# The second down-projection of a ConvFFN as seven block products per pair of output tiles

## The chip, the cores and the metric

One Trainium2 chip, one of its NeuronCores. The metric is the device time of one execution in microseconds (us); shown is the median of several runs. TensorE (PE) multiplies, VectorE (DVE), ScalarE (ACT) and GpSimd (POOL) work elementwise, SyncE (SP) issues most of the DMA transfers. The engines run side by side, each through its own program in order, and meet only at semaphores.

## The reference

One layer of a hybrid recurrent decoder with a convolutional feed-forward network, over 1056 tokens: a prompt of 1024 and 8 samples of 4. Everything is float32. What matters here is its end:

```python
h2 = modulate(h_res, p['g_ffn'], sh2, sc2)
up = h2 @ p['w_up']                                   # 1024 -> 2 x 2816
buf = jnp.concatenate([st_conv[layer], up], axis=1)
conv = causal_dwconv(buf, p['conv_w'], p['conv_b'], l) # three taps in time
a_ff, b_ff = jnp.split(conv, 2, axis=-1)
h_res = h_res + gt2[:, None, :] * ((jax.nn.gelu(a_ff) * b_ff) @ p['w_down'])   # 2816 -> 1024
...
y = rms_norm(h_res, final_g).astype(x.dtype)
```

## The kernel before

All activations are held transposed: channels on the 128 partitions, the 1056 tokens along the free dimension. Up to the end of the token mixers and the output projection the change touches nothing.

The feed-forward network runs in two halves over its 22 channel tiles of 128, `HALVES = ((0, 12), (12, 22))`. In each half, the up-projection makes for every step `r` one tile of `a_ff` and one of `b_ff`; the gated result is stored tile by tile in `FFh`. Then the down-projection adds this half's contribution to the residual. So the second half's down-projection has ten k tiles (channels 12 to 21).

The up-projection and the output projection are already done in blocks: a 2 x 2 block matrix product with seven block products in the place of eight (Winograd's form of Strassen's method). The weights of a step are four blocks A11 to A22 (two output tiles, two halves of the k tiles), the activations four blocks B11 to B22 (two halves of the k tiles, two halves of 528 tokens). VectorE makes the weight sums S1 = A21 + A22, S2 = S1 - A11, A11 - A21 (in the place of A21 in the weight slot) and S4 = A12 - S2 (`four_sums`), and the activation sums once for the whole stage. TensorE does the products in PSUM banks, taken in pairs, and VectorE and ScalarE combine them from there (`combined` in the up-projection). Each product is two groups of 264 columns.

The down-projection of both halves is done plainly: for each of eight output tiles, three token groups of 352 columns, each summed over the k tiles in one PSUM bank out of six (`gemm`). The first tile begins with the k tiles that are ready and ends with the last two (`gemm_from_early`), which the convolution of the last step still works on. VectorE adds each group to the residual with the gate (`residual`), and in the second half also accumulates the squares for the final norm and scales by its gain (`squares(2, m)`).

On VectorE, a step of the up-projection is: the convolution `conv(r-1, 0)` of the step before (three taps for 1024 prompt tokens, three for the 32 decode tokens), the combination of product 2, `conv(r-1, 1)`, which also multiplies with the GELU branch and signals `ff_ready`, then the combinations of products 4 and 5, weight sums for the next step around the latter, and the combinations of products 6 and 7. The two convolutions of a half's last step come behind its last combination. Its signals are counted: the banks of the last step's first and third product are free with the combination of product 6, those of its second with that of product 7.

Weights come in chunks through two slots of `W`. SyncE loads chunk i when TensorE has finished with chunk i - 2 (`weights`); a chunk of the second down-projection is 1280 KB and holds two output tiles. Behind the second of these chunks SyncE reloads the residual, eight tiles of 528 KB, from `xres` into `xT`, which shares its memory with the up-projection's activation sums.

Behind the last residual, TensorE sums the squares over the partitions (`sq3`, two planes, against a column of ones), VectorE and ScalarE make the reciprocal root, TensorE turns the tiles into rows, VectorE and ScalarE scale these out of PSUM, and SyncE stores them.

Every instruction of VectorE's `step` signals its end, and the engine waits for it. L718 is TensorE's matrix product helper, L722 its transposition, L2001 VectorE's tensor-tensor, L2004 its scalar-tensor-tensor, L2592 the first tap of the convolution, L2060 the scaling by the final gain, L439 SyncE's weight load, L536 its reload of the residual.

Of the kernel before, what the change touches and what calls it, by code (L numbers as in the profile page):

```python
# [15 lines left out]
P = 128  # L16
D = 1024
KT = D // P
# [3 lines left out]
T = TP + TS  # L22
# [3 lines left out]
G, GW = 3, T // 3  # L26
# [48 lines left out]
def weight_chunks():  # L75
# [10 lines left out]
    for m0, m1 in HALVES:  # L86
        out += [("up", m, 2 * PRODUCTS) for m in range(m0, m1, 2)]
        out += [("down", (m0, c), 2 * G) for c in range(4)]
    return out


def trunk(nc, I, O):
# [5 lines left out]
    with ctx:  # L98
# [160 lines left out]
        sq2, rstd2 = carve(18944, 2, T), carve(21056, T)  # L259
        sq3 = carve(21056, 2, T)  # L260

# [134 lines left out]
        def product(r, x):  # L396

            return signals[index[("up", 2 * (r // 2))]] + PRODUCTS * (r % 2) + x

        def slots(r):  # L400
# [302 lines left out]
        def _(pe):  # L703
# [790 lines left out]
            def last_rows(n):  # L1494
# [6 lines left out]
                give("conv_rows", 7)  # L1501

            def pair(r):

# [36 lines left out]
            for half, (m0, m1) in enumerate(HALVES):  # L1541
# [13 lines left out]
                pe.wait_ge(sem("ff_ready"), m1 - 2)  # L1555
                for c in range(4):
                    i = index[("down", (m0, c))]
# [34 lines left out]
        def _(act):  # L1592
# [359 lines left out]
            for m0, m1 in HALVES:  # L1952
# [18 lines left out]
                decode_rows(m1 - 1)  # L1971
                state_rows(m1 - 1)
            rows_out(FT // 2 - 1)
            root(rs9, 12)
# [9 lines left out]
        def _(dve):  # L1984
# [622 lines left out]
            dve.wait_ge(sem("x_in0"), 64 + 16 * KT)  # L2607
            def second_half(m, from_):

                gt, d = MOD[:, 16 + m, :], dec4(res_t[:])  # L2610
                x = xT[:, m, HT:TP]
                step(stt(x, from_[:, 0:TP - HT], gt[:, 0:1], x, MUL, ADD))
                step(tt(d, dec4(from_[:, TP - HT:HT]), gt[:, 1:].unsqueeze(2).to_broadcast([P, NS, LS]), MUL))
                return tt(xT[:, m, TP:T], xT[:, m, TP:T], res_t[:], ADD)

            def first_half(m, from_):
                x = in_two(xT[:, m, 0:HT])
                return stt(x, from_, MOD[:, 16 + m, 0:1], x, MUL, ADD)

# [50 lines left out]
            for half, (m0, m1) in enumerate(HALVES):  # L2670
                for r in range(m0, m1):
# [12 lines left out]
                    if r + 1 < m1:  # L2684
                        sums(r + 1, 2, 4)
                    combined(r, 6, c21, c21, x, SUB)
                    combined(r, 7, c12, c12, y, ADD)
# [7 lines left out]
                else:  # L2695
                    for k in range(2):
                        dve.wait_ge(sem(f"x_in{k}"), (320, 208)[k])
                    residual(signals[index[("down", (m0, 0))]], 40, 2)
            step(v.memset(rs9, 1.0))
# [47 lines left out]
```

## Time and profile before

| | |
|---|---|
| median of 3 runs | 2348.9 us |
| lowest and highest | 2346.8, 2354.57 us |
| profiled execution: its time | 2351.13 us |
| profiled execution: its span | 2349.4 us |
| mean granted clock of TensorE | 0.984 |
| busy: TensorE, VectorE, ScalarE, GpSimd | 2243.8, 1069.8, 403.0, 162.2 us |

The span is from the first to the last instruction of one execution; its time has some more around it. "Busy" is the sum of the intervals in which an engine works; several engines are busy at once. The granted clock is the share of TensorE's full clock that the chip let it have: 1.00 is 2.4 GHz, 0.50 is 1.2 GHz. In the timelines a line is a run of like instructions of one engine, merged, and the bracket behind it tells the idle time of its engine before it and what ended that.

### The profile page before, as it was taken

Reading aid. Unit: us, or ns where it says so; the run is one execution under the profiler, and the core shown is the slowest. Engines: PE = TensorE matmul, PEld = TensorE weight load, DVE = VectorE, ACT = ScalarE, POOL = GpSimd, SP = SyncE. Lnnn points to the kernel's source line nnn. Section 1 sums busy time; section 2 is a strip of 40 time slices with the busy share of each in tenths; the row PEclk is TensorE's granted clock in tenths of the full one; section 3 lists DMA queues with packets and bytes.
Section 4 is the critical chain, followed back from the end, with each engine's and each line's share of the span. In section 5 each row is a group of like instructions: output and inputs, shape, how many; then the busy total and the mean of one; then the engine's idle time right before and its main releaser. Section 6 shows DMA issues by size and latency. Waiting matters only on the chain.

```text
span 2349.4 us, 41778 instructions
## 1 busy us (share of the span) xinstructions
PE 2243.8 (96%) x18567; PEld 1601.7 (68%) x18567; DVE 1069.8 (46%) x1698; ACT 403.0 (17%) x775; POOL 162.2 (7%) x276
## 2 busy tenths in 40 slices
PE   5998999998999999899889998999999999999998
PEld 4665666566567566566656686888886668888666
DVE  5775334252353253234234656666652115566423
ACT  3124121231132042132110003111110001111001
POOL 2610000001002002001000000000000000000000
PEclk8999999999999999999999999999999999999999
DMA  8200232212021111211236322111112231110301
GB/s 315 79 23 11 65 123 88 72 47 57 20 67 32 49 31 51 63 37 47 69 112 213 101 74 73 37 38 38 38 60 77 82 109 38 37 39 24 119 23 75
DMA packets 117090, 161.52 MB, mean 69 GB/s; under 512 B 15442, under 2 KB 86599, under 8 KB 116896
## 3 DMA queue, kind: packets, MB, share of 16 engines
q1 hardware_dynamic: 101120, 132.68, 17.1%
q10 hardware_dynamic: 10992, 15.21, 1.8%
q0 software_dynamic: 4800, 10.97, 1.4%
q8 instruction: 147, 2.41, 0.4%
q14 instruction: 31, 0.25, 0.0%
HBM read 126.24 MB, written 32.59 MB: 68 GB/s over the span
## 4 chain that ended last, share of the span: by engine, by line
PE 92%; DMA 3%; ACT 2%; DVE 1%; issue 1%; SPq 1%; POOL 0%; DVEq 0%; ACTq 0%
PE ps L718 91%; DMA W<-in_w_in_dram 2%; PE ps L722 1%; ACT Y L1704 1%; DVE arena L2001 1%; SPq L424 1%; DVE hT L2001 0%; SPq L439 0%; DMA arena<-in_state_s_dram 0%; ACT hT L1906 0%; DMA out_dram<-arena 0%; ACT hT L1647 0%; DVE arena L2189 0%; ACT L1704 0%; SPq L443 0%
## 5 line engine op out<-in xcount | busy, mean ns | idle before, releaser
L718 PE MATMUL ps<-hT,W 128*128 128x352 f32 (+1 forms) x3376 | 1002.6, 447 | 26.9 <-DMA W<-in_w_in_dram 13.0
L718 PEld LDWEIGHTS ps<-hT,W 128*128 128x128 f32 x3376 | 632.9, 192 | 287.0 <-issue 23.1
L718 PE MATMUL ps<-arena 64*64 64x64 f32 (+8 forms) x9784 | 414.3, 240 | 37.2 <-issue 20.4
L718 PEld LDWEIGHTS ps<-arena 64*64 64x64 f32 (+4 forms) x9784 | 332.6, 138 | 166.7 <-issue 100.8
L718 PE MATMUL ps<-arena,W 128*128 128x352 f32 (+1 forms) x1600 | 439.4, 434 | 1.6 <-DVE arena L2001 1.6
L718 PEld LDWEIGHTS ps<-arena,W 128*128 128x128 f32 x1600 | 303.9, 190 | 131.2 <-issue 2.1
L2001 DVE TENSOR_TENSOR arena<-ps,arena 128x512 f32<-128x512 f32 (+4 forms) x124 | 93.2, 751 | 243.6 <-PE ps L718 199.1
L2001 DVE TENSOR_TENSOR Y<-Y,ps 128x528 f32<-128x528 f32 x130 | 91.6, 705 | 241.6 <-PE ps L718 241.5
L2001 DVE TENSOR_TENSOR arena<-arena 128x1056 f32<-128x1056 f32 (+6 forms) x178 | 159.9, 898 | 63.7 <-PE ps L718 48.9
L1602 ACT ACTIVATE Y<-ps 128x528 f32<-128x528 f32 (+1 forms) x92 | 37.5, 407 | 804.8 <-DVE Y L2001 293.3
L1602 ACT ACTIVATE arena<-ps 128x512 f32<-128x512 f32 (+6 forms) x143 | 86.9, 617 | 457.6 <-PE ps L718 269.1
L2004 DVE SCALAR_TENSOR_TENSOR arena<-ps,MOD,arena 128x352 f32<-128x352 f32 (+2 forms) x52 | 30.5, 587 | 241.5 <-PE ps L718 236.2
L650 POOL DMA_DIRECT2D out_dram<-arena x72 | 40.4, 567 | 1334.0 <-ACT arena L1602 1061.0
L718 PE MATMUL ps<-Y,W 128*128 128x352 f32 x384 | 114.7, 460 | 5.2 <-DVE Y L2001 2.7
L718 PEld LDWEIGHTS ps<-Y,W 128*128 128x128 f32 x384 | 72.6, 190 | 46.0 <-DVE Y L2001 3.2
L1730 ACT ACTIVATE arena<-ps 128x352 f32<-128x352 f32 x72 | 33.5, 465 | 323.0 <-PE ps L718 323.0
L671 POOL TENSOR_TENSOR arena<-arena,m_lt 128x512 f32<-128x512 f32 x40 | 50.4, 1267 | 399.0 <-DVE flag L2428 281.6
L2004 DVE SCALAR_TENSOR_TENSOR Y<-Y,PAR 128x1024 f32<-128x1024 f32 (+1 forms) x88 | 67.6, 768 | 3.1
L2004 DVE SCALAR_TENSOR_TENSOR arena<-Y,PAR,arena 128x1024 f32<-128x1024 f32 (+1 forms) x88 | 67.6, 768 | 3.1
L718 PEld LDWEIGHTS ps<-idS,arena 64*64 64x64 f32 (+1 forms) x1888 | 40.3, 134 | 26.1 <-issue 20.9
L718 PE MATMUL ps<-hT,arena 128*128 128x264 f32 x240 | 55.9, 386 | 0.0
L718 PEld LDWEIGHTS ps<-hT,arena 128*128 128x128 f32 x240 | 45.6, 190 | 7.8
(295 smaller groups left out, 1353.3 us busy)
## 6 DMA issues: line engine op xcount, KB each, us to landing
W<-in_w_ada_dram SPq DMA_DIRECT2D x12, 2048.0 KB, 9.6
W<-in_w_up_dram SPq DMA_DIRECT2D x22, 1024.0 KB, 7.1
W<-in_w_in_dram SPq DMA_DIRECT2D x13, 1024.0 KB, 6.3
gates<-arena ACTq DMA_DIRECT2D x72, 176.0 KB, 1.8
arena<-gates SPq DMA_DIRECT2D x24, 528.0 KB, 3.7
arena<-xres SPq DMA_DIRECT2D x24, 528.0 KB, 5.2
xres<-arena POOLq DMA_DIRECT2D x16, 528.0 KB, 5.8
W<-in_w_in_dram SPq DMA_DIRECT2D x13, 512.0 KB, 7.3
```

The source lines that it names most:

```text
L424: sp.dma_start(dst, src).then_inc(sem("small_in"), 16)
L650: pool.dma_start(dst, src).then_inc(sem(name), 16)
L671: pool.tensor_tensor(LT[:, 8 * s:8 * s + 8, :], LA[:, 8 * s:8 * s + 8, 0, :], m_lt[:, l, :].unsqueeze(1).to_broadcast([P, 8, RCH]), MUL)\
L718: return nc.tensor.matmul(out, lhsT, rhs, start=start, stop=stop, skip_group_check=True)
L722: return nc.tensor.transpose(out, in_, ident[0:n, 0:n])
L1602: return nc.scalar.activation(out, in_, ACT.Copy)
L1704: m = nc.scalar.activation(Y[q, j // 4, o::DS], src[32 * o:32 * o + 32, 0:M], ACT.Gelu_apprx_tanh)
L1730: nc.scalar.activation(stage, bank[:, 0:GW], ACT.Sigmoid).then_inc(sem("gate_ev"), 1)
L2001: return v.tensor_tensor(out, a, b, op)
L2004: return v.scalar_tensor_tensor(out=out, in0=a, scalar=s, in1=b, op0=op0, op1=op1)
```

## The change

The second half's down-projection is done in blocks as well. Its ten k tiles are two halves of five, its 1056 tokens two halves of 528, and each of the four weight chunks (two output tiles) is four blocks of 5 x 128 columns. Per chunk (a pair r) there are seven block products of five k tiles and two groups of 264 columns (`down_pair`).

- VectorE makes the activation sums once: FT1 = F12 - F11 and the first pair's four weight sums between the combinations of products 5 and 6 of the up-projection's last step; FT2 = F22 - FT1, FT3 = F22 - F12 and FT4 = FT2 - F21 (in the place of F12) behind the last two convolutions.
- TensorE's products in a pair: 1 A11 F11 (banks 0, 1), 2 S1 FT1 (banks 2, 3), 3 A12 F21 onto 1, 4 S2 FT2 (banks 4, 5), 5 (A11 - A21) FT3 (banks 0, 1), 6 A22 FT4 (banks 4, 5), 7 S4 F22 onto 2. Each waits for its sums and for the reader of its banks. F21 and F22 hold the last two channel tiles (`ff_ready`).
- ScalarE copies product 1 to SBUF (`p12_ev`). VectorE adds the products up and adds the results to the residual (`down_blocks_out`): u2 = product 1 + product 4, v = u2 + product 5, and so on, with the next pair's weight sums between them, and squares and scaling of the two tiles at the pair's end. In the last pair these are cut into halves of the tokens and ordered so that little follows the last product.
- The activation sums, weight sums and partial results lie in `hT`, which held the normed input of the up-projection, and in free parts of `Y` and the arena. `sq3` moves from the arena to `Y`.
- The chunks now count 7 signals instead of 6, so SyncE's loads wait for the seventh product of a pair.

The diff, its core:

```diff
--- before.py
+++ after.py
@@ -85,7 +85,7 @@
     out += [("out", c, 2 * PRODUCTS) for c in range(2)]
     for m0, m1 in HALVES:
         out += [("up", m, 2 * PRODUCTS) for m in range(m0, m1, 2)]
-        out += [("down", (m0, c), 2 * G) for c in range(4)]
+        out += [("down", (m0, c), PRODUCTS if m0 else 2 * G) for c in range(4)]
     return out
...
@@ -257,7 +257,7 @@
         cvr = carve(23168, 2, 512)
...
-        sq3 = carve(21056, 2, T)
+        sq3 = Yf[:, T:3 * T].rearrange("p (a b) -> p a b", a=2)
...
@@ -396,6 +396,25 @@
         def product(r, x):
 
             return signals[index[("up", 2 * (r // 2))]] + PRODUCTS * (r % 2) + x
+
+        KH = (HALVES[1][1] - HALVES[1][0]) // 2
+        five = lambda a: a.rearrange("p (k c) -> p k c", k=KH)
+        F11, F12, F21, F22 = (FFh[:, KH * a:KH * (a + 1), HT * b:HT * (b + 1)] for a in range(2) for b in range(2))
+        FT1a, FT1b = carve(21056, 4, HT), Yf[:, 7088:7088 + HT]
+        FT2, FT3, FT4 = five(hflat[:, 0:KH * HT]), five(hflat[:, KH * HT:2 * KH * HT]), F12
+        SD = [[five(a) for a in (carve(8448, KH * P), carve(8448 + KH * P, KH * P), Yf[:, 7616:7616 + KH * P])],
+              [five(hflat[:, 5280 + KH * P * i:5280 + KH * P * (i + 1)]) for i in range(3)]]
+        dpart = [hflat[:, 7200:7200 + HT], hflat[:, 7200 + HT:7200 + 2 * HT], Yf[:, 0:HT]]
+        S_DOWN, P12_DOWN, RES_DOWN = 16 + 4 * FT, 4 + 2 * FT, 28 + KT * G
+
...
@@ -1500,6 +1519,50 @@
...
+            def down_pair(r):
+
+                def multiply_down(b, A, B, first=True, last=True):
+                    for g in range(2):
+                        for k in range(KH):
+                            m = mm(pb[b + g][:, 0:HG], A[:, k, :], B(k)[:, HG * g:HG * (g + 1)],
+                                   first and k == 0, last and k == KH - 1)
+                    m.then_inc(sem("gemm_done"), 1)
+
+                arrived(index[("down", (HALVES[1][0], r))])
+                A11, A12, A21, A22 = down_blocks(r)
+                S1, S2, S4 = SD[r % 2]
+                of = lambda B: lambda k: B[:, k, :]
+                take(0, 1)
+                multiply_down(0, A11, of(F11), True, False)
+                pe.wait_ge(sem("s_sums"), S_DOWN + 4 * r + 1)
+                if r == 0:
+                    pe.wait_ge(sem("h_ready"), 5)
+                take(2, 3)
+                multiply_down(2, S1, lambda k: FT1a[:, k, :] if k < 4 else FT1b, True, False)
+                if r == 0:
+                    pe.wait_ge(sem("ff_ready"), FT)
+                pe.wait_ge(sem("p12_ev"), P12_DOWN + r + 1)
+                multiply_down(0, A12, of(F21), False, True)
+                pe.wait_ge(sem("s_sums"), S_DOWN + 4 * r + 2)
+                if r == 0:
+                    pe.wait_ge(sem("h_ready"), 6)
+                take(4, 5)
+                multiply_down(4, S2, of(FT2))
+                pe.wait_ge(sem("s_sums"), S_DOWN + 4 * r + 3)
+                if r == 0:
+                    pe.wait_ge(sem("h_ready"), 7)
+                pe.wait_ge(sem("res_ev"), RES_DOWN + 7 * r + 1)
+                multiply_down(0, A21, of(FT3))
+                if r == 0:
+                    pe.wait_ge(sem("h_ready"), 8)
+                pe.wait_ge(sem("res_ev"), RES_DOWN + 7 * r + 2)
+                multiply_down(4, A22, of(FT4))
+                pe.wait_ge(sem("s_sums"), S_DOWN + 4 * r + 4)
+                pe.wait_ge(sem("res_ev"), RES_DOWN + 7 * r + 4)
+                multiply_down(2, S4, of(F22), False, True)
+                for b, at in ((0, 3), (4, 5), (2, 6)):
+                    last_read[b] = last_read[b + 1] = ("res_ev", RES_DOWN + 7 * r + at)
+
...
@@ -1553,7 +1616,10 @@
...
                 pe.wait_ge(sem("ff_ready"), m1 - 2)
-                for c in range(4):
+                if half:
+                    for r in range(4):
+                        down_pair(r)
+                for c in range(0 if half else 4):
...
@@ -1970,6 +2036,11 @@
...
+            for r in range(4):
+                act.wait_ge(sem("gemm_done"), down_product(r, 1))
+                if r:
+                    act.wait_ge(sem("res_ev"), RES_DOWN + 7 * r)
+                copy(in_two(dpart[0]), ps[:, 0:2, 0:HG]).then_inc(sem("p12_ev"), 1)
...
+            def down_sums(r, lo, hi):
+
+                i = index[("down", (HALVES[1][0], r))]
+                dve.wait_ge(sem(f"w_in{i % 2}"), loads[i])
+                four_sums(down_blocks(r), SD[r % 2], lo, hi)
+
+            def down_blocks_out():
+
+                one, acc = sq3[:, 0, :], sq3[:, 1, :]
+
+                def scaled(m, cols):
+                    x = xT[:, m, cols]
+                    return v.tensor_scalar(x, x, par("final_g", m), None, MUL)
+
+                def added_square(m, cols):
+                    x = xT[:, m, cols]
+                    step(tt(one[:, cols], x, x, MUL))
+                    step(tt(acc[:, cols], acc[:, cols], one[:, cols], ADD))
+
+                dve.wait_ge(sem("cob_made"), 2 * FT)
+                for k in range(2):
+                    dve.wait_ge(sem(f"x_in{k}"), (320, 208)[k])
+                u2, v_, c22 = (in_two(a) for a in dpart)
+                x, y, z = (ps[:, b:b + 2, 0:HG] for b in (0, 2, 4))
+                for r in range(4):
+                    m, last = 2 * r, r == 3
+                    dve.wait_ge(sem("p12_ev"), P12_DOWN + r + 1)
+                    dve.wait_ge(sem("gemm_done"), down_product(r, 3))
+                    step(first_half(m, x, 40), "res_ev")
+                    if last:
+                        added_square(m, slice(0, HT))
+                        step(scaled(m, slice(0, HT)))
+                    dve.wait_ge(sem("gemm_done"), down_product(r, 4))
+                    step(tt(u2, u2, z, ADD), "res_ev")
+                    if not last:
+                        down_sums(r + 1, 0, 2)
+                    dve.wait_ge(sem("gemm_done"), down_product(r, 5))
+                    step(tt(v_, u2, x, ADD), "res_ev")
+                    step(tt(c22, v_, y, ADD), "res_ev")
+                    if not last:
+                        down_sums(r + 1, 2, 4)
+                    dve.wait_ge(sem("gemm_done"), down_product(r, 6))
+                    step(tt(v_, v_, z, SUB), "res_ev")
+                    step(first_half(m + 1, v_, 40))
+                    step(second_half(m + 1, dpart[2], 40))
+                    if last:
+                        step(tt(one, xT[:, m + 1, :], xT[:, m + 1, :], MUL))
+                    dve.wait_ge(sem("gemm_done"), down_product(r, 7))
+                    step(tt(u2, u2, y, ADD), "res_ev")
+                    step(second_half(m, dpart[0], 40), "res_ev")
+                    if not last:
+                        squares(2, m)
+                        squares(2, m + 1)
+                rest = slice(HT, T)
+                step(tt(c22, in_two(xT[:, KT - 2, rest]), in_two(xT[:, KT - 2, rest]), MUL))
+                step(tt(acc[:, rest], acc[:, rest], dpart[2], ADD), "acc_ready")
+                step(scaled(KT - 2, rest), "xn_ready")
+                step(scaled(KT - 1, slice(0, T)), "xn_ready")
 
...
@@ -2683,6 +2813,10 @@
                     combined(r, 5, c22, c21, y, ADD)
                     if r + 1 < m1:
                         sums(r + 1, 2, 4)
+                    elif half:
+                        down_sums(0, 0, 4)
+                        step(tt(FT1a, F12[:, 0:4], F11[:, 0:4], SUB))
+                        step(tt(FT1b, F12[:, 4], F11[:, 4], SUB), "h_ready")
                     combined(r, 6, c21, c21, x, SUB)
                     combined(r, 7, c12, c12, y, ADD)
...
                 else:
-                    for k in range(2):
-                        dve.wait_ge(sem(f"x_in{k}"), (320, 208)[k])
-                    residual(signals[index[("down", (m0, 0))]], 40, 2)
+                    step(tt(FT2[:, 0:4], F22[:, 0:4], FT1a, SUB))
+                    step(tt(FT2[:, 4], F22[:, 4], FT1b, SUB), "h_ready")
+                    step(tt(FT3, F22, F12, SUB), "h_ready")
+                    step(tt(FT4, FT2, F21, SUB), "h_ready")
+                    down_blocks_out()
```

## Rows read from the trace of the kernel before

**Rows 1.** The page: busy time of the engines, and the chain that ended last.
```profile
PE 2243.8 (96%) x18567; PEld 1601.7 (68%) x18567; DVE 1069.8 (46%) x1698; ACT 403.0 (17%) x775; POOL 162.2 (7%) x276
...
PE 92%; DMA 3%; ACT 2%; DVE 1%; issue 1%; SPq 1%; POOL 0%; DVEq 0%; ACTq 0%
```

**Rows 2.** Stages: us, busy us (instructions) of PE, PEld, DVE, ACT, POOL, clock, DMA.
```profile
1975.00:2182.80 207.80, 207.80 (x950) 176.49 (x949) 125.73 (x181) 27.52 (x92) 8.07 (x16) 1.00 0.12 39
2182.80:2324.80 142.00, 142.00 (x482) 91.10 (x481) 49.20 (x72) 1.01 (x8) 0.00 (x0) 1.00 0.16 59
2324.80:2349.40 24.60, 15.71 (x113) 14.99 (x111) 10.20 (x19) 8.50 (x13) 2.53 (x4) 0.80 0.46 178
```

**Rows 3.** Timeline of TensorE from 2179: start, length, what.
```profile
2179.21 3.72 PE L718 MATMUL ps<-hT,Y 128*128 128x264 f32 x16
2182.77 142.16 PE L718 MATMUL ps<-arena,W 128*128 128x352 f32 x480
2324.77 0.60 PE L722 MATMUL ps<-ident,Y 128*18 128x128 f32 x4
2327.51 5.47 PE L718 MATMUL ps<-ones,arena 128*128 128x1 f32 x36 [2.14 <-DVE flag L2056]
```

**Rows 4.** Timeline of VectorE from product 5's combination to the first residual.
```profile
2175.92 0.71 DVE L2001 TENSOR_TENSOR Y<-Y,ps 128x528 f32<-128x528 f32 x1 [2.86 <-PE ps L718]
2179.48 0.70 DVE L2001 TENSOR_TENSOR Y<-Y,ps 128x528 f32<-128x528 f32 x1 [2.85 <-PE ps L718]
2183.04 0.70 DVE L2001 TENSOR_TENSOR Y<-Y,ps 128x528 f32<-128x528 f32 x1 [2.85 <-PE ps L718]
2183.78 0.81 DVE L2592 TENSOR_SCALAR Y<-Y,PAR 128x1024 f32<-128x1024 f32 x1
...
2193.86 1.26 DVE L2001 TENSOR_TENSOR arena<-arena,Y 128x1056 f32<-128x1056 f32 x1
2200.28 1.79 DVE L2004 SCALAR_TENSOR_TENSOR arena<-ps,MOD,arena 128x352 f32<-128x352 f32 x3 [5.16 <-DMA arena<-xres]
```

**Rows 5.** VectorE's groups by shape from 1430 on: busy time, mean ns.
```profile
L2001 DVE TENSOR_TENSOR Y<-Y,ps 128x528 f32<-128x528 f32 x112 | 78.9, 705 | 215.1 <-PE ps L718 215.1
...
L2001 DVE TENSOR_TENSOR arena<-arena 128x1056 f32<-128x1056 f32 x14 | 17.6, 1258 | 0.5
L2001 DVE TENSOR_TENSOR W<-W 128x512 f32<-128x512 f32 x21 | 14.5, 692 | 0.7
...
L2001 DVE TENSOR_TENSOR arena<-hT 128x2112 f32<-128x2112 f32 x2 | 4.7, 2359 | 3.0 <-ACT hT L1906 2.9
...
L2004 DVE SCALAR_TENSOR_TENSOR arena<-Y,MOD,arena 128x528 f32<-128x528 f32 x1 | 0.8, 769 | 0.0
```

**Rows 6.** DMA issues from 2182 to 2262: size of each, us to landing.
```profile
W<-in_w_down_dram SPq DMA_DIRECT2D x3, 1280.0 KB, 5.9
```

**Rows 7.** Timeline of VectorE: the last residual, and the output projection's end.
```profile
1435.85 0.70 DVE L2001 TENSOR_TENSOR Y<-Y,ps 128x528 f32<-128x528 f32 x1 [2.61 <-PE ps L718]
1436.59 0.73 DVE L2004 SCALAR_TENSOR_TENSOR arena<-Y,MOD,arena 128x496 f32<-128x496 f32 x1
...
1437.58 0.19 DVE L2001 TENSOR_TENSOR arena<-arena,res_t 128x32 f32<-128x32 f32 x1
...
2325.04 0.55 DVE L2004 SCALAR_TENSOR_TENSOR arena<-ps,MOD,arena 128x320 f32<-128x320 f32 x1 [5.33 <-PE ps L718]
```

**Rows 8.** Timeline of TensorE: groups behind idle times.
```profile
1217.96 7.34 PE L718 MATMUL ps<-Y,W 128*128 128x352 f32 x24 [2.71 <-DVE Y L2001]
...
1444.19 6.12 PE L718 MATMUL ps<-hT,W 128*128 128x264 f32 x16 [4.40 <-issue]
...
1459.11 5.49 PE L718 MATMUL ps<-arena 128*128 128x264 f32 x16 [4.21 <-DVE arena L2001]
```

**Rows 9.** Busy time and clock of the stretches behind these idle times.
```profile
1444.20:1450.30 6.10, 6.10 (x16) 4.53 (x16) 5.82 (x9) 2.77 (x4) 0.00 (x0) 0.62 0.41 164
1459.10:1464.40 5.30, 5.29 (x16) 4.32 (x17) 4.92 (x7) 0.00 (x0) 0.00 (x0) 0.68 0.01 3
1218.00:1225.30 7.30, 7.30 (x24) 4.41 (x24) 0.01 (x1) 0.71 (x2) 2.50 (x4) 1.00 0.75 258
```

More of the change, by code:

```diff
@@ L398, in product, with down_blocks, down_product @@
             return signals[index[("up", 2 * (r // 2))]] + PRODUCTS * (r % 2) + x
+        KH = (HALVES[1][1] - HALVES[1][0]) // 2
[7 more added lines that the diff above has]
+        S_DOWN, P12_DOWN, RES_DOWN = 16 + 4 * FT, 4 + 2 * FT, 28 + KT * G
+        def down_blocks(r):
+            w = wslot(index[("down", (HALVES[1][0], r))], 0, 2 * KH, 256)
+            return [w[:, KH * b:KH * (b + 1), P * a:P * (a + 1)] for a in range(2) for b in range(2)]
+        def down_product(r, x):
+            return signals[index[("down", (HALVES[1][0], r))]] + x
         def slots(r):
@@ L2607, in _, with second_half @@
             dve.wait_ge(sem("x_in0"), 64 + 16 * KT)
-            def second_half(m, from_):
-                gt, d = MOD[:, 16 + m, :], dec4(res_t[:])
+            def second_half(m, from_, gate=16):
+                gt, d = MOD[:, gate + m, :], dec4(res_t[:])
                 x = xT[:, m, HT:TP]
@@ L2614, in second_half, with first_half @@
                 return tt(xT[:, m, TP:T], xT[:, m, TP:T], res_t[:], ADD)
-            def first_half(m, from_):
+            def first_half(m, from_, gate=16):
                 x = in_two(xT[:, m, 0:HT])
-                return stt(x, from_, MOD[:, 16 + m, 0:1], x, MUL, ADD)
+                return stt(x, from_, MOD[:, gate + m, 0:1], x, MUL, ADD)
+            def down_sums(r, lo, hi):
+                i = index[("down", (HALVES[1][0], r))]
+                dve.wait_ge(sem(f"w_in{i % 2}"), loads[i])
+                four_sums(down_blocks(r), SD[r % 2], lo, hi)
```

## The prediction

> **What bounds the kernel now.** I read the page first: TensorE is busy for 96% of the span and 92% of the chain that ended last runs over it [rows 1]. So a change can only pay by giving TensorE less to do, and what it gives VectorE to do costs only where TensorE has to wait for it. Then the table by stage: in the second half's up-projection and in its down-projection TensorE is busy all of the time at a granted clock of 1.00, while VectorE is busy for 125.7 of 207.8 us and for 49.2 of 142.0 us [rows 2]. The timeline of TensorE gives the stage that is replaced: it starts at 2182.77, right behind the last block product of the up-projection (16 records in 3.56 us from start to start), and ends where the four small transposes start, at 2324.77; after that there are 2.14 us of idle time, the row sums of squares from 2327.51 and the last transposes [rows 3]. Last, the timeline of VectorE around the junction, since the change puts VectorE in front of TensorE there: it is loaded right up to it, and the convolutions of the last two channel tiles end only at 2195.12, 12.4 us after the down-projection has begun [rows 4]. The present form hides this: it begins with the k tiles that are ready and has 8 of 10 of them to chew on for three token groups. Only afterwards does VectorE wait, until 2200.28, for the residual, which holds nobody up.
>
> **What TensorE saves.** Before: 8 output tiles x 3 groups x 10 k tiles = 240 matrix products of 352 columns in 142.00 us, 0.592 us each (two records each, 480 in all) [rows 3]. After: 4 pairs x 7 products x 2 groups x 5 k tiles = 280 of 264 columns. The up-projection's block products have the same width and do 8 in 3.56 us, so 0.445 us each [rows 3], and a product of five k tiles takes 4.45 us. 28 of them take 124.6 us. Gain if TensorE never waits: 17.4 us. The weight loads stay hidden, as they do in the up-projection at this width (clock and busy time of its stage are full) [rows 2].
>
> **What VectorE gets at the junction.** Its tensor-tensor operations cost 0.692 us at 512 elements and 2.358 at 2112, 1.04 ns for each element more [rows 5]; about 0.035 us pass between two. So a weight sum of 5 x 128 = 640 elements takes 0.83 us, one of 528 takes 0.71, the sum of five tiles (2640) takes 2.91. The trace has neither 640 nor 2640: the first lies between the rows of 512 and 1056 (0.69 and 1.26), the second is at least 2.36; I take the line through the rows, which fits the 1056 row too.
>
> Ahead of the convolutions, between the combination of product 5 and that of product 6, stand four weight sums (4 x 0.86), FT1's four tiles (2.39) and its fifth (0.74): 6.57 us. Product 5's combination ends at 2176.63 [rows 4], so they end at 2183.2. The combination of product 6, at 2179.48 before, then ends at 2183.95, that of product 7 at 2184.7. Two things hang on this. TensorE's banks 0 and 1 come free only with the combination of product 6, so the first product starts at about 2184.05 in place of 2182.77: **1.3 us**. And the two convolutions start 0.93 late and end at 2196.05.
>
> Product 1 (A11 F11) runs to 2188.5, product 2 (S1 FT1) to 2192.95. The third needs F21, which holds the last two channel tiles, and waits for all of them: it starts at about 2196.15, **3.2 us** of idle TensorE. ScalarE's copy of product 1 (an ACTIVATE of 528 from PSUM takes 0.61) is done long before. Product 3 ends at 2200.6, product 4 at 2205.05. In this time VectorE makes FT2 (3.12), FT3 (2.94), FT4 (2.94): ready at 2199.2, 2202.1 and 2205.1. FT2 and FT3 are in time for products 4 and 5. But product 5 goes into the banks that the first residual half still reads, and that addition stands behind FT4 in VectorE's order: 2205.1 + 0.77 [rows 5] and the signal give 2205.95, **0.9 us**. From then on products 5 to 7 of the pair end at 2219.3. In all 5.4 us of TensorE's time are exposed of 15.6 us of added VectorE work.
>
> The reload of the residual is not in this: SyncE issues it at the same event as before, it has landed by 2200.28 [rows 4], and VectorE now asks for it at 2205.1.
>
> **The other three pairs.** TensorE needs 31.15 us for a pair. VectorE's work in it: 5 combinations and the two halves of two tiles (about 8 us with the decode columns), 4 weight sums (3.4), two tiles' squares and scaling (2 x 3.4): 18 us. Every bank is read at least one product (4.45 us) before it is wanted again, and the squares (6.8 us after product 7) end before product 3 of the next pair does. The weights: chunk r+1 can only be loaded when pair r-1 is through, and VectorE wants it after product 4 of pair r, 17.8 us later; 1280 KB landed in 5.9 [rows 6]. So no waits: 21 x 4.45 = 93.5, and product 28 ends at 2312.75, against 2324.77: 12.0 us gained.
>
> **The end.** Before, VectorE's last residual starts at 2325.04 and TensorE's sums of squares at 2327.51 [rows 3, 7]: 2.47. Now what follows the last product is u2 + y (0.74), a second half of a tile (0.77 + 0.22 + 0.22), the square of 528 (0.74) and the addition (0.75): 3.45. The same pieces stand in the trace after the output projection, 1435.85 to 1437.77 for the first two [rows 7]. **1.0 us** lost. The scaling (1.3 us) lies beneath the sums of squares (5.4 us). Net: 17.4 - 1.3 - 3.2 - 0.9 - 1.0 = 11.0.
>
> **The clock.** This trace shows what an idle TensorE can cost. After 2.71 us of idle time 12 matrix products of 352 ran in 7.34 us, at clock 1.00; after 4.21 us a block product took 5.49 in place of 3.72, after 4.40 it took 6.12, with the mean clock of these stretches at 0.68 and 0.62, part of them at 1.2 GHz [rows 8, 9]. The new gap of 3.2 us lies between. If the clock falls there, products 3 and 4 take 1.8 us more, of which the 0.9 us wait behind FT4 absorbs half: 0.8 net. I call it even and take 0.4. The same holds for the end, where the clock was at 1.2 GHz for a part of the sums and transposes already (mean 0.80 over the stage [rows 2]); the gap there grows from 2.1 to about 3.1 us. I leave it equal, with 1.8 us either way.
>
> Where VectorE and TensorE take turns on a few banks, one rule speaks against the change: the Trainium skill, "TensorE: Matmul & The Clock Gate", section "A second HAM failure mode: psum-queue depth-cycling", says that a matmul stream which cycles through PSUM banks can pause often enough for its clock to swing between its two levels. The up-projection here does just that, and its row shows clock 1.00; by that row the rule costs nothing, by the rule the result would be rival 3.
>
> Sum: 11.0 - 0.4 = 10.6 us. The profiled execution is 2351.1 around a span of 2349.4; it lies 2.2 above the median of the runs, 2348.9. I take the difference from the median: **2338.3**.
>
> **Rivals.**
> 1. *The junction is fully hidden.* Then 17.4 - 1.0 = 16.4 and 2332.5. Against it: the third product's input ends at 2195.12 even with nothing added [rows 4], 3.5 us after two products that start at 2182.77. Chance 0.05, for savings that I don't see, such as a clock that stays up at the end.
> 2. *The junction is fully exposed*: all 15.6 us of added VectorE work stand before TensorE, since FT2 to FT4 and the convolutions follow each other. 17.4 - 15.6 - 1.0 = 0.8: 2348.1. For it: one VectorE does all in order. Against it: 4 products of 4.45 run beside it. Chance 0.04.
> 3. *The clock falls once in each pair*, in pauses at the banks. At 1.8 to 2.4 us for each of four [rows 8]: 7 to 10 us given back, 2345 to 2348. It would need pauses of some 4 us; I find none after the first pair. Chance 0.04.
> 4. *Slower: weight chunks late.* The loads of the third and fourth chunk lose half of their lead, since seven products use a chunk to the end in 31 us, and the sums want it before the pair begins. A load later than 17.8 us first holds up VectorE's sums, and from about 23 us, when the combination of product 5 comes too late for product 7, TensorE. Two such loads give back all 10.6 us from a landing time of 29 us on; at 33 us the kernel takes 2357.5, slower. Against it: 5.9 us measured, with nothing else in the queue by then. Chance 0.03.
> 5. *The change doesn't do what it says*: products of five tiles that run slower than those of four, at 142.0 / 280 = 0.507 us in place of 0.445 TensorE saves nothing, and with 6.4 us of waits the result is 2355. Same width, same operand memories; chance 0.01.
>
> **How the numbers follow.** The forecast has a chance of 0.83, with a range of its own of 2335 to 2341 (clock at the junction up or down 0.4, clock at the end 1.8, a median of runs that spread over 8 us). The whole range goes to rival 1 on the one side and into rival 3 on the other: 2333 to 2345. Faster by over 0.3% (7 us; about what this kernel's measurement can tell from no change) means below 2341.9: the forecast and rival 1, 0.88. Within 0.3%: rivals 2 and 3, 0.08. Slower: 0.04.
>
> **What the profile after would show.** TensorE: 28 products at 4.45 us apart; three gaps, about 1.3 us before the first product (ended by VectorE's combination), 3.2 before the third (by the last convolution), 0.9 before the fifth (by the first residual half), and no other until the end of pair 4. VectorE: four sums of 640 at 0.83 and FT1 at 2.36 ahead of the combination of product 6. At the end 3.4 us from VectorE's first addition to the sums of squares. The prediction is wrong if TensorE waits again in pairs 2 to 4, if products run at another rate than 0.445 us a piece with the clock up, or if the clock stays low for longer than the two pairs of products that I allow it.

## The result, and the profile after

The changed kernel takes **2337.64 us** (median of 5 runs, 2335.07 to 2339.77) against 2348.9 before; the ratio is 0.9946, with a 95% interval of 0.9929 to 0.9963. It is faster by 11.3 us by the medians; forecast were 2338.3 and a gain of 10.6. The profiled execution has a span of 2333.4 us, 16.0 less than the one shown of before. That is more than the change did; where the rest comes from is in the first experiment.

The page of the changed kernel, busy time and the chain that ended last, to be held against [rows 1]:

```profile
PE 2226.3 (95%) x18647; PEld 1617.3 (69%) x18647; DVE 1106.8 (47%) x1734; ACT 404.3 (17%) x779; POOL 161.4 (7%) x276
...
PE 91%; DMA 3%; DVE 2%; ACT 2%; issue 1%; SPq 1%; POOL 0%; DVEq 0%; ACTq 0%
```

TensorE is busy 17.5 us less, VectorE 37 us more, and TensorE is still the bound. That 17.5 lies so near the 17.4 of the prediction is chance: within the stage TensorE is busy 126.80 us in place of 142.00, which is 15.2 less, and the rest arose ahead of it, where the change does nothing. The timeline of TensorE through the stage (answers to [rows 3]; the line numbers have moved, L737 is L718 of before, L2072 is L2001):

```profile
2174.11 3.72 PE L737 MATMUL ps<-hT,Y 128*128 128x264 f32 x16
2179.09 4.69 PE L737 MATMUL ps<-arena,W 128*128 128x264 f32 x20 [1.26 <-DVE Y L2072]
...
2191.01 6.41 PE L737 MATMUL ps<-arena,W 128*128 128x264 f32 x20 [2.78 <-DVE arena L2072]
2197.26 4.61 PE L737 MATMUL ps<-hT,arena 128*128 128x264 f32 x20
2201.71 4.61 PE L737 MATMUL ps<-hT,W 128*128 128x264 f32 x20
...
2304.06 4.61 PE L737 MATMUL ps<-arena,hT 128*128 128x264 f32 x20
2308.51 0.60 PE L741 MATMUL ps<-ident,Y 128*18 128x128 f32 x4
2312.24 5.56 PE L737 MATMUL ps<-ones,Y 128*128 128x1 f32 x36 [3.14 <-DVE Y L2072]
```

The stage begins where the up-projection's last product ends, at 2174.11 + 3.56 = 2177.67, and ends with the small transposes at 2308.51: **130.84 us, where it took 142.00**. Product 1 waits 1.26 us, product 3 waits 2.78, and product 3 itself takes 6.25 from start to start instead of 4.45: the clock fell. From product 5 at 2201.71 on, 24 products take 106.8 us, 4.45 each, without a gap. TensorE's waits between 2177 and 2309 are these two:

```profile
PE ps L737 <- DVE arena L2072: 2.8, 1, 2.8
PE ps L737 <- DVE Y L2072: 1.3, 1, 1.3
```

The busy time by stretch, around the gap and then for the rest of the four pairs (columns as in [rows 2]; the last three figures are granted clock, DMA share and GB/s):

```profile
2180.00:2191.00 11.00, 8.23 (x37) 6.68 (x36) 10.50 (x15) 1.28 (x7) 0.00 (x0) 1.00 1.04 398
2191.00:2197.30 6.30, 6.29 (x21) 5.09 (x22) 6.20 (x4) 0.00 (x0) 0.00 (x0) 0.73 0.42 169
...
2219.50:2250.70 31.20, 31.20 (x142) 26.64 (x141) 15.98 (x22) 0.61 (x1) 0.00 (x0) 1.00 0.14 43
2250.70:2281.80 31.10, 31.10 (x141) 26.56 (x140) 17.11 (x24) 0.61 (x1) 0.00 (x0) 1.00 0.03 10
2281.80:2308.50 26.70, 26.70 (x121) 22.70 (x120) 13.03 (x18) 0.61 (x1) 0.00 (x0) 1.00 0.00 0
```

The clock is 0.73 in the mean while product 3 runs: it was still at 1.00 through the idle time before it (2188.3 to 2191.0), fell to 0.50 within the product's first 0.5 us, and was back at 1.00 from 2195 on, before the product ended. It is 1.00 in pairs 2 to 4, where VectorE is busy for about half of the time. The timeline of VectorE at the junction, against [rows 4]:

```profile
2170.82 0.70 DVE L2072 TENSOR_TENSOR Y<-Y,ps 128x528 f32<-128x528 f32 x1 [2.86 <-PE ps L737]
2171.56 0.82 DVE L2072 TENSOR_TENSOR arena<-W 128x640 f32<-128x640 f32 x1
...
2175.00 2.36 DVE L2072 TENSOR_TENSOR arena<-arena 128x2112 f32<-128x2112 f32 x1
...
2178.13 1.44 DVE L2072 TENSOR_TENSOR Y<-Y,ps 128x528 f32<-128x528 f32 x2
...
2189.70 1.26 DVE L2072 TENSOR_TENSOR arena<-arena,Y 128x1056 f32<-128x1056 f32 x1
...
2194.13 2.91 DVE L2072 TENSOR_TENSOR hT<-arena 128x2640 f32<-128x2640 f32 x1
2197.07 2.91 DVE L2072 TENSOR_TENSOR arena<-hT,arena 128x2640 f32<-128x2640 f32 x1
2200.01 0.77 DVE L2075 SCALAR_TENSOR_TENSOR arena<-ps,MOD,arena 128x528 f32<-128x528 f32 x1
```

There is no pause in it: combination of product 5, four weight sums and FT1, then the combinations of products 6 and 7 together at 2178.13, with which TensorE's first product comes free; the last convolution's multiplication ends at 2190.96, and product 3 starts at 2191.01; FT3 and FT4; the first residual half ends at 2200.78, in time for product 5 only because TensorE was 1.8 us slower. The shapes of 640 and 2640 elements take 0.82 and 2.91 us.

### The profile page after: what moved, and what is told of

It is laid out like the page before. It is cut to its first block, busy times and chain, and to the rows that moved or that the text cites. A ratio compares the mean times of both kernels' runs of the same rounds, so it can differ in the third digit from the quotient of the medians.

```text
span 2333.4 us, 42007 instructions
## 1 busy us (share of the span) xinstructions
PE 2226.3 (95%) x18647; PEld 1617.3 (69%) x18647; DVE 1106.8 (47%) x1734; ACT 404.3 (17%) x779; POOL 161.4 (7%) x276
## 3 DMA queue, kind: packets, MB, share of 16 engines
q1 hardware_dynamic: 101120, 132.68, 17.4%
## 4 chain that ended last, share of the span: by engine, by line
PE 91%; DMA 3%; DVE 2%; ACT 2%; issue 1%; SPq 1%; POOL 0%; DVEq 0%; ACTq 0%
PE ps L737 90%; DMA W<-in_w_in_dram 2%; PE ps L741 1%; DVE arena L2072 1%; ACT Y L1770 1%; SPq L443 1%; DVE hT L2072 0%; DMA arena<-in_state_s_dram 0%; SPq L458 0%; DVE Y L2072 0%; DVE Y L2075 0%; ACT hT L1972 0%; DMA out_dram<-arena 0%; ACT hT L1713 0%; ACT L1770 0%
## 5 line engine op out<-in xcount | busy, mean ns | idle before, releaser
L737 PE MATMUL ps<-hT,W 128*128 128x352 f32 (+1 forms) x3456 | 1016.4, 444 | 27.6 <-DMA W<-in_w_in_dram 16.1
L737 PEld LDWEIGHTS ps<-hT,W 128*128 128x128 f32 x3456 | 646.3, 192 | 289.5 <-issue 21.9
L737 PE MATMUL ps<-arena 64*64 64x64 f32 (+6 forms) x9816 | 420.3, 239 | 36.0 <-issue 19.2
L737 PEld LDWEIGHTS ps<-arena 64*64 64x64 f32 (+3 forms) x9816 | 337.1, 138 | 164.2 <-issue 95.9
L737 PE MATMUL ps<-arena,W 128*128 128x264 f32 (+1 forms) x1360 | 354.5, 419 | 5.7 <-DVE arena L2072 4.4
L737 PEld LDWEIGHTS ps<-arena,W 128*128 128x128 f32 x1360 | 259.3, 191 | 93.6 <-issue 3.8
L2072 DVE TENSOR_TENSOR arena<-ps,arena 128x512 f32<-128x512 f32 (+4 forms) x124 | 93.2, 751 | 243.0 <-PE ps L737 198.8
L2072 DVE TENSOR_TENSOR Y<-Y,ps 128x528 f32<-128x528 f32 x130 | 91.5, 704 | 236.1 <-PE ps L737 235.9
L2072 DVE TENSOR_TENSOR arena<-arena 128x1056 f32<-128x1056 f32 (+6 forms) x165 | 144.6, 876 | 60.1 <-PE ps L737 45.7
L737 PE MATMUL ps<-Y,W 128*128 128x352 f32 x384 | 114.7, 460 | 4.8 <-DVE Y L2072 2.7
L737 PEld LDWEIGHTS ps<-Y,W 128*128 128x128 f32 x384 | 72.6, 190 | 45.6 <-DVE Y L2072 3.2
L2075 DVE SCALAR_TENSOR_TENSOR arena<-ps,MOD,arena 128x352 f32<-128x352 f32 (+2 forms) x32 | 19.9, 621 | 165.7 <-PE ps L737 165.7
L737 PE MATMUL ps<-hT,arena 128*128 128x264 f32 x280 | 65.1, 386 | 0.0
L737 PEld LDWEIGHTS ps<-hT,arena 128*128 128x128 f32 x280 | 53.2, 190 | 9.1
L737 PEld LDWEIGHTS ps<-idS,arena 64*64 64x64 f32 (+1 forms) x1888 | 40.3, 134 | 26.1 <-issue 20.9
```

The costliest lines, as they stand in the source:

```text
L737: return nc.tensor.matmul(out, lhsT, rhs, start=start, stop=stop, skip_group_check=True)
L2072: return v.tensor_tensor(out, a, b, op)
L2075: return v.scalar_tensor_tensor(out=out, in0=a, scalar=s, in1=b, op0=op0, op1=op1)
```

## The experiments

All stage times are taken like the 130.84 above: from the end of the up-projection's last product to the start of the small transposes. A stage time comes out alike to 0.02 us from execution to execution of one program where the clock does the same (experiments 1, 2 and 9), so one profile of each version can be compared. Whether the clock falls behind a given idle time is known for experiments 3 to 8 from one execution each.

**1. The changed kernel again, and once more later.** No edit.

> The changed kernel once more, as the measure of what two executions of one program differ by. Stage time here and below: from the end of the up-projection's last block product (its start + 3.56 us) to the start of the four small transposes behind product 28; 130.8 us in the profile after, 142.0 before. Expected if the stage is set by the program: 130.8 again where the clock falls at the junction, 130.0 where it does not, whatever the whole span does. The span may differ by several us, since 5 of the 16 us between the two profiled spans arose ahead of the change. If instead the change had moved something earlier in the program, the marker where the up-projection ends would lie 5 us earlier again.

> The changed kernel, on the same chip and in the same rounds: ratio to the kernel before between 0.9946 and 0.9962, 9 to 13 us faster; stage 130.8 or 130.0 by the clock at the junction.

Measured: stage 130.83 (2180.50 to 2311.33) and 130.84 (2179.30 to 2310.14), with the clock falling at product 3 both times. Spans 2336.3 and 2335.1; medians 2339.47 and 2338.5, ratios 0.9962 (0.9947 to 0.9977) and 0.9955 (0.9939 to 0.9971). By the medians of its three sets of runs the changed kernel is 11.3, 8.6 and 11.0 us faster. The stage repeats, the whole time only to some us.

**2. The kernel before again.**

> The kernel before, for a second profile of it: stage 142.0 to a tenth, sums 2.7 us behind it. The span is expected some 2 to 3 us from the first profile's 2349.4, with the difference ahead of the second up-projection or in the clock of the end, not in the stage. If the first profile's stage had been a lucky or unlucky one, it differs here.

The timeline of TensorE:

```profile
2174.42 3.72 PE L718 MATMUL ps<-hT,Y 128*128 128x264 f32 x16
2177.98 142.16 PE L718 MATMUL ps<-arena,W 128*128 128x352 f32 x480
2319.98 0.60 PE L722 MATMUL ps<-ident,Y 128*18 128x128 f32 x4
2322.73 5.14 PE L718 MATMUL ps<-ones,arena 128*128 128x1 f32 x36 [2.15 <-DVE flag L2056]
```

Stage 142.00 again. The span is 2344.3, which is 5.1 less than the first profile's, where 2 to 3 were expected; 4.8 of these lie ahead of the stage, which begins at 2177.98 in place of 2182.77. Over all fourteen profiled executions of this study, with TensorE's program the same up to there, it begins between 2177.7 and 2185.3. With this the 16.0 us between the two profiled spans resolve: 5.1 ahead of the stage, which is within what executions of one program differ by (4.6 of it are there already at the group at 1217.96 in [rows 8], far ahead of the change, which starts at 1213.38 in the changed kernel's profile); 11.2 in it; 1.0 lost in front of the sums of squares; 0.7 gained behind, by the clock (21.16 us from the sums to the end, 21.89 before).

**3. The gap before product 3 filled.** Six products that nobody reads, in bank 6:

```diff
+                    take(6)
+                    for k in range(6):
+                        mm(pb[6][:, 0:HG], A11[:, k % KH, :], F11[:, k % KH, 0:HG], k == 0, k == 5)
                     pe.wait_ge(sem("ff_ready"), FT)
```

> Six unused matrix products (264 columns, into a bank that nobody reads) fill the idle time before product 3 of the first pair; nothing else changes. If that idle time is what makes the clock fall, product 3 takes 4.45 us in place of 6.25 at clock 1.00, but product 5 then waits for the first residual half behind FT4 until 23.2 us into the stage, in place of 24.0: stage 130.0. If the clock falls for another reason (the level of the whole stage), product 3 stays at about 6.2 and the stage at 130.8.

```profile
2188.26 7.67 PE L737 MATMUL ps<-arena,W 128*128 128x264 f32 x32
2195.76 4.61 PE L737 MATMUL ps<-hT,arena 128*128 128x264 f32 x20
2201.13 4.69 PE L737 MATMUL ps<-hT,W 128*128 128x264 f32 x20 [0.75 <-DVE arena L2078]
...
2191.30:2195.70 4.40, 4.40 (x20) 3.78 (x21) 4.33 (x3) 0.00 (x0) 0.00 (x0) 1.00 0.58 226
```

The 32 records are the filler (12) and product 3 (20); the last line is the stretch of product 3, at clock 1.00. Product 4 starts at 2195.76, 17.90 us into the stage, where product 3 at full clock ends; with the idle time filled and the rest as before, the residual's reload beside it too, the clock did not fall, so the idle time was what had let it. And now the wait behind FT4 that the forecast had for product 5 is there, 0.75 us by TensorE's row. Stage 130.14. So of the 1.8 us of slow clock 0.7 reach the end, as long as FT4 stands behind it.

**4. The filler, and FT4 moved** from ahead of the first residual half to behind the addition of product 4:

```diff
-                    step(tt(FT4, FT2, F21, SUB), "h_ready")
                     down_blocks_out()
...
                     step(tt(u2, u2, z, ADD), "res_ev")
+                    if r == 0:
+                        step(tt(FT4, FT2, F21, SUB), "h_ready")
```

> The filler of before, and FT4 moved on VectorE from ahead of the first residual half to behind the addition of product 4. With the clock up and FT4 out of the way, product 5 starts when product 4 ends, 22.3 us into the stage (23.2 with the filler alone), and FT4 is ready at 26.2, before product 6 wants it at 26.7: stage 129.1. If something else than FT4 held product 5, it stays at 130.1.

```profile
2204.56 4.61 PE L737 MATMUL ps<-hT,W 128*128 128x264 f32 x20
```

This is product 5, 22.35 us into the stage and without a wait. Stage 129.15, and no wait for TensorE from product 3 to 28. What held product 5 was VectorE's order, not the work. FT4 moved without the filler or the split was not run.

**5. Sums spread out.** Two weight sums behind the combination of product 4, two and FT1's fifth tile behind that of 5, FT1's four tiles behind that of 6:

```diff
+                    elif half:
+                        down_sums(0, 0, 2)
                     combined(r, 5, c22, c21, y, ADD)
...
                     elif half:
-                        down_sums(0, 0, 4)
-                        step(tt(FT1a, F12[:, 0:4], F11[:, 0:4], SUB))
-                        step(tt(FT1b, F12[:, 4], F11[:, 4], SUB), "h_ready")
+                        down_sums(0, 2, 4)
+                        step(tt(FT1b, F12[:, 4], F11[:, 4], SUB))
                     combined(r, 6, c21, c21, x, SUB)
+                    if half and r + 1 == m1:
+                        step(tt(FT1a, F12[:, 0:4], F11[:, 0:4], SUB), "h_ready")
```

> The first pair's weight sums and FT1 are spread over VectorE's idle times between the last step's combinations 4 to 7. If VectorE's order sets the junction: no wait before product 1 (1.3 before), last convolution ends at 12.35 into the stage in place of 13.3, product 3 starts at 12.4 behind 3.5 us of idle time; with the clock falling there product 5 starts at 23.15, stage 129.9 (129.0 if it does not fall). If product 1 waits for something else (weights), nothing moves: 130.8.

```profile
2180.34 4.61 PE L737 MATMUL ps<-arena,W 128*128 128x264 f32 x20
...
2192.75 6.41 PE L737 MATMUL ps<-arena,W 128*128 128x264 f32 x20 [3.35 <-DVE arena L2072]
```

No wait before product 1, product 3 at 12.41 us into the stage behind 3.35 us idle, the clock falls again; stage 129.90. The first wait was VectorE's sums, and they had room beside TensorE.

**6. The same sums late**, between the last combination and the last two convolutions:

```diff
                     combined(r, 7, c12, c12, y, ADD)
+                if half:
+                    down_sums(0, 0, 4)
+                    step(tt(FT1a, F12[:, 0:4], F11[:, 0:4], SUB))
+                    step(tt(FT1b, F12[:, 4], F11[:, 4], SUB), "h_ready")
                 conv(m1 - 1, 0)
```

> The opposite: the same sums and FT1 stand behind the last combination, between it and the last two convolutions. Product 1 starts at 0, product 2 at 7.6, the last convolution ends at 18.9, product 3 starts at 19.0 behind 6.9 us of idle time, product 5 at 28.9 to 30: stage 135.7 to 137. If the 6.6 us of sums could hide anywhere on VectorE, the stage would stay within 1 us of 130.8.

```profile
2184.41 4.61 PE L737 MATMUL ps<-arena,W 128*128 128x264 f32 x20
2192.06 3.86 PE L737 MATMUL ps<-arena 128*128 128x264 f32 x8 [3.04 <-issue]
...
2203.40 6.41 PE L737 MATMUL ps<-arena,W 128*128 128x264 f32 x20 [3.78 <-DVE arena L2072]
```

Product 2 at 7.65, product 3 at 18.99, stage **136.49**; half of the change's gain is gone through the place of six VectorE instructions. The clock fell twice, for product 2 and again in product 3. The first fall made product 2 some 3 us longer, so that the idle time before product 3 was 3.78 us and not the 6.9 of the expectation; it did not delay product 3, which waits for the last convolution either way.

**7. Product 3 split by k tiles.**

```diff
-                if r == 0:
-                    pe.wait_ge(sem("ff_ready"), FT)
                 pe.wait_ge(sem("p12_ev"), P12_DOWN + r + 1)
-                multiply_down(0, A12, of(F21), False, True)
+                if r == 0:
+                    for k0, k1 in ((0, KH - 2), (KH - 2, KH)):
+                        if k0:
+                            pe.wait_ge(sem("ff_ready"), FT)
+                        for g in range(2):
+                            for k in range(k0, k1):
+                                m = mm(pb[g][:, 0:HG], A12[:, k, :], F21[:, k, HG * g:HG * (g + 1)],
+                                       False, k == KH - 1)
+                    m.then_inc(sem("gemm_done"), 1)
+                else:
+                    multiply_down(0, A12, of(F21), False, True)
```

> Product 3 of the first pair is split by k tiles: the three that are ready first, the last two behind the wait for the convolutions. If only the wait for the last two channel tiles cost time, the 2.7 us of work that now lie in the gap and the 1.8 us of slow clock are both gained: product 5 starts near 19.6 us into the stage, 126.4 in all. If VectorE's order behind it is the next bound, product 4 waits for FT2 until 16.5, and product 5 for the first residual half behind FT4 until 23.2 (24.0 in the changed kernel): stage 130.0.

```profile
2201.84 4.69 PE L737 MATMUL ps<-hT,arena 128*128 128x264 f32 x20 [1.13 <-issue]
2208.57 6.38 PE L737 MATMUL ps<-hT,W 128*128 128x264 f32 x20 [2.04 <-DVE arena L2083]
```

Expected 130.0, measured **131.81**: a miss. The starts came as worked out, product 4 at 16.52 and product 5 at 23.25 us into the stage. But at product 5 the clock fell, behind 2.04 us of idle time with 1.13 us more ahead of product 4, and it took 6.21 us. The split alone moved the gap to a place where nothing hides the slow clock. I had counted only on longer gaps for a fall. Without the fall product 5 would have taken 4.45 us, and the stage by that estimate the 130.0 expected; this is one execution, and whether another falls at this gap too is not known.

**8. The split and FT4 moved.** Both edits above.

> Product 3 split by k tiles and FT4 moved, together. FT3 is ready at 19.4 and the first residual half at 20.2, product 4 ends at 20.95 and product 5 starts there; FT4 at 24.9 is in time for product 6 at 25.4. Stage 127.7, 3.1 us less than the changed kernel. The rival, that the two changes gain no more than the better one alone, gives 129.1 or more.

```profile
2201.25 4.69 PE L737 MATMUL ps<-hT,arena 128*128 128x264 f32 x20 [1.13 <-issue]
2205.78 4.61 PE L737 MATMUL ps<-hT,W 128*128 128x264 f32 x20
```

Stage 127.84, product 5 at 21.04, right behind product 4, and the clock stays at 1.00. Together they gain 3.0 us, where the one loses 1.0 and the other, with the filler, gains 1.7.

**9. All three edits**, twice.

> All three: sums and FT1 spread over the idle times, product 3 split, FT4 moved. Product 1 without a wait, convolutions done at 12.35, product 4 starts with FT2 at 15.5, product 5 at 20.0: stage 126.8, 4.0 us less than the changed kernel and 15.2 less than the kernel before, with 2.2 us of waits left against 28 products without any (124.6). Device time some 4 us below the changed kernel, near 2334; ratio to the kernel before 0.994.

> The version with all three edits once more, beside the next two on one chip: stage 126.9; device time between 2333 and 2337, 2 to 4 us below the changed kernel if the 3.9 us of the stage show in it, none if they are lost in what executions differ by.

Stage 126.93 and 126.92. The timeline of the first:

```profile
2181.09 4.61 PE L737 MATMUL ps<-arena,W 128*128 128x264 f32 x20
...
2193.51 2.05 PE L737 MATMUL ps<-arena,W 128*128 128x264 f32 x8 [0.69 <-DVE arena L2080]
2196.69 4.69 PE L737 MATMUL ps<-hT,arena 128*128 128x264 f32 x20 [1.14 <-issue]
```

Medians 2335.1 and 2334.5, ratios 0.9939 (0.9924 to 0.9954) and 0.9935 (0.9918 to 0.9951). Beside the changed kernel in the same rounds (2338.5, 0.9939 to 0.9971) the medians say 4.0 us, what the stage says, but the intervals overlap: shown is the stage, not the whole. Both beat the kernel before.

**10. The end filled too**: seven products that nobody reads between the small transposes and the sums of squares.

```diff
+            for k in range(7):
+                mm(pb[6][:, 0:HG], ones[:], F22[:, k % KH, 0:HG], k == 0, k == 6)
             pe.wait_ge(sem("acc_ready"), 4)
```

> The version with all three edits, and seven unused matrix products (3.1 us) in TensorE's idle time between the four small transposes and the sums of squares. Stage 126.9 as before it. If the idle time there makes the clock fall at once, the 36 sums take 3.9 to 5.6 us in place of 7.3 and sums and transposes together (18.1 in the last execution, 15.1 to 17.9 over the executions so far) 15.2 or less. If the clock falls whatever TensorE did just before, since sums of one column and transposes don't hold it, the two together stay between 15.1 and 18.1.

```profile
2312.64 3.28 PE L737 MATMUL ps<-arena,ones 128*128 128x264 f32 x14
2315.94 5.33 PE L737 MATMUL ps<-ones,Y 128*128 128x1 f32 x36
2321.20 9.89 PE L741 MATMUL ps<-ident,arena 128*128 128x128 f32 x72
```

The clock over the sums' first stretch and the next:

```profile
2316.00:2318.00 2.00, 2.00 (x19) 2.00 (x19) 1.25 (x3) 0.00 (x0) 0.00 (x0) 1.00 0.03 8
2318.00:2320.00 2.00, 2.00 (x12) 2.00 (x12) 0.00 (x0) 0.00 (x0) 0.00 (x0) 0.53 0.00 0
```

Stage 126.91; sums and transposes together 15.2 us. Both outcomes on record contain this value: without the filler they took between 15.1 and 18.2 us in the profiles of versions with the longer gap. The clock stayed up until the sums had begun and fell in them all the same. Device time 2333.8, ratio 0.9938 (0.9919 to 0.9956), the same as without it. Whether the filler is worth having stays open.

## Why the prediction was right

- **28 products at 4.45 us.** Right to the hundredth: 24 of them in 106.8 us at clock 1.00.
- **VectorE's operations.** 0.83 and 2.91 us were taken for shapes that the trace did not have; measured 0.82 and 2.91.
- **Three waits.** Forecast 1.3, 3.2 and 0.9 us, the last if the clock did not fall. Product 1 and product 3 started 1.42 and 13.34 us into the stage, forecast 1.28 and 13.38. (Product 1 started 0.14 later and took 4.53, so the gap before product 3 was 2.94 us by the starts, and 2.78 in the row, where the modelled end of product 2 lies 0.16 later.) The third wait was absorbed by the slow clock, and stands in the filled version with 0.75.
- **The clock.** This was taken as even odds, 0.8 us net if it fell: product 5 started 24.04 us into the stage, where 23.18 was worked out for no fall, so 0.86 net. It fell in all three profiles of this form, and in product 3 alone (6.25 us), not in 3 and 4; product 4 took 4.45. The 0.4 in the sum was the mean of two outcomes; with the outcome that came, 0.8, the stage gains 11.2, as measured.
- **The end.** 1.0 us forecast, measured 2308.51 to 2312.24 = 3.73 against 2.74 before. The rows:

```profile
2308.78 0.70 DVE L2072 TENSOR_TENSOR hT<-hT,ps 128x528 f32<-128x528 f32 x1 [0.43 <-PE ps L737]
...
2310.74 0.71 DVE L2072 TENSOR_TENSOR Y<-arena 128x528 f32<-128x528 f32 x1
2311.48 0.71 DVE L2072 TENSOR_TENSOR Y<-Y 128x528 f32<-128x528 f32 x1
```

 That the clock at the end is equal for both is not so clear. From the sums to the end the two profiles of before took 21.89 and 21.57 us; eleven with the longer gap took 21.2 to 23.5, 22.5 in the mean. Some 0.8 us may be lost there, within the 1.8 allowed; with two profiles against eleven that is not settled.
- **Sum.** 17.4 - 1.3 - 3.2 - 0.9 - 0.8 - 1.0 = 10.2 us by the steps with the fall of the clock, 10.2 (11.16 - 0.99) by the traces, 11.3 by the medians. The interval of the ratio means 9 to 17 us, and the later sets gave 8.6 and 11.0; so that the median came within 0.7 us of the forecast is in part luck. What the runs bear out is the stage, to 0.1 us once the clock's fall is known.
- **The rivals.** The junction neither hidden (1) nor fully exposed (2): the stage took 130.84 against 124.6 for 28 products without a wait, so with 15.6 us of added VectorE work 6.2 us were lost, the clock's share among them. The late version shows that the place of 6.6 us of sums alone moves the stage by 5.7. A fall of the clock in each pair (3): pairs 2 to 4 run at 1.00. Late weights (4): no wait was for them, and they landed in 5.9 us again:

```profile
W<-in_w_down_dram SPq DMA_DIRECT2D x3, 1280.0 KB, 5.9
```

- Slower products (5): none.
- The rule of the Trainium skill in "TensorE: Matmul & The Clock Gate", section "A second HAM failure mode: psum-queue depth-cycling", describes a matmul stream that cycles through PSUM banks and idles so often between its groups that the clock swings. It did not come about here: 24 products through three pairs of banks ran without a pause at clock 1.00 over 106.8 us. Since there were no pauses between them, this says nothing of what short pauses would do. The clock fell where TensorE had waited for VectorE's results.

## What to carry to other kernels

When a block form replaced this plain matrix product, the gain could be read beforehand from a neighbour of the same width (4.45 us for a product, forecast and measured); what it cost was at the seam, where the sums meet work that the old form could begin without. Lay the other engine's instructions out in time from the last thing before the seam, with the trace's durations, and ask of each product which one it waits for: here it gave every start that was forecast within 0.15 us, but for product 5 of the changed kernel itself, which the fallen clock made 0.9 us later. Then look for idle slots of that engine before the seam and for sums that stand ahead of something wanted sooner; moving six instructions was worth from minus 5.7 to plus 0.9 us, and all three reorderings 3.9, all of the stage.

## What the runs showed of the hardware

**Whether an idle time lets TensorE's clock fall differs between executions of one program.** The wait of 2.7 us ahead of 24 records of 352 columns, at 1217.96 in [rows 8], is in every profile. These are its rows in the changed kernel's first profile and in its second:

```profile
1213.38 7.34 PE L737 MATMUL ps<-Y,W 128*128 128x352 f32 x24 [2.70 <-DVE Y L2072]
```

```profile
1216.62 9.03 PE L737 MATMUL ps<-Y,W 128*128 128x352 f32 x24 [2.70 <-DVE Y L2072]
```

Of the twelve profiles in which these 24 records stand alone, six show 7.34 us, five 9.03, one 8.77. In the other two they are merged with the 12 behind them, and the clock over the first 4 us or so is 0.61 and 0.50, so it fell in 8 of 14. The prediction took the 7.34 of one trace as a sign that such a gap is safe. A gap of 2.04 us with 1.13 ahead of it was not (clock 0.72 over the product behind it), and in front of product 2 or 3 gaps of 2.78 to 3.78 us let the clock fall each of the six times. A forecast should give such a gap a chance of a fall, and 1.7 to 1.8 us as its price for the records behind it. What of this reaches the end depends on the next wait: the 12 records behind these 24 start 9.4 to 10.0 us after them whether the clock fell or not, and at the junction 0.7 of 1.8 us came through.

**The clock at the end.** It falls in or before the 36 one-column sums in every profile. Where it fell before them, they took 7.3 us, where in their course, 5.1 to 6.5; this alone moves the span by some 2 us from one execution to the next.
